# Gate chain of an mLSTM and MoE layer divided anew between engines, with a moved product, other banks, one transpose per tile and another load order

## The reference, cut to what matters

```
h = rmsnorm(x, g_pre_mix) * (1.0 + scale_a) + shift_a
z = h @ w_in                                  # u | q | k | v | o | gate_pre
pre = gate_pre + b_gate
log_i, log_f = pre[i], jax.nn.log_sigmoid(pre[f])     # per direction, head, token
...
b = jnp.cumsum(log_f); m_t = jnp.maximum(b + m, max(b_t - b_s + log_i_s))
p = jnp.exp(d_intra - m_t) * (q @ k)
...
mix = jnp.concatenate([y_pool, y_ml]) @ w_out
x = x + gate_a * rmsnorm(mix, g_post_mix)
x = x + gate_f * rmsnorm(moe(...), g_post_ffn)        # 64 experts, top 6
```

## Time and profile before

| | us |
|---|---|
| median of 3 runs | 725.98 (725.54 to 726.65) |
| the profiled execution | 726.23 |
| its span | 724.10 |
| PE busy, share of the span | 685.0 (95%) |
| DVE, ACT, POOL busy | 384.5, 194.1, 89.1 |
| mean granted TensorE clock | 0.994 of full speed |

### The profile page before, as it was taken

How to read it: one execution, slowest core, us unless ns; L and a number is a source line. 1 busy time by engine, 2 the same in 40 slices (tenths; PEclk the granted TensorE clock), 3 DMA queues, 4 the chain that set the end, 5 groups by cost and what they waited for, 6 DMA issues and landing times.

```text
span 724.1 us, 11495 instructions
## 1 busy us (share of the span) xinstructions
PE 685.0 (95%) x4263; PEld 395.1 (55%) x4263; DVE 384.5 (53%) x979; ACT 194.1 (27%) x335; POOL 89.1 (12%) x53
## 2 busy tenths in 40 slices
PE   2799999989999999999999999999999999999993
PEld 2588888767865735545444545454445445444431
DVE  3458989694298354454444445454445436442115
ACT  3245344563371302112111111211111121130103
POOL 2453655313213000000000000000000000000000
PEclk9999999999999999999999999999999999999997
DMA  9999875815489479999999999999999999999994
GB/s 316 382 350 340 260 245 221 296 55 175 146 329 426 204 290 417 428 423 427 393 386 428 421 425 424 423 425 424 425 424 427 423 425 426 423 426 421 419 410 189
DMA packets 51013, 259.16 MB, mean 358 GB/s; under 512 B 6704, under 2 KB 9312, under 8 KB 32904
## 3 DMA queue, kind: packets, MB, share of 16 engines
q1 hardware_dynamic: 46816, 252.50, 86.6%
q0 software_dynamic: 1584, 4.90, 2.0%
q10 hardware_dynamic: 2552, 0.98, 0.5%
HBM read 254.64 MB, written 3.71 MB: 357 GB/s over the span
## 4 chain that ended last, share of the span: by engine, by line
PE 66%; DMA 14%; DVE 12%; SPq 3%; issue 2%; ACT 2%; POOL 0%; DVEq 0%; ACTq 0%
PE psum L2495 22%; PE psum L2503 10%; PE psum L2383 9%; PE psum L2467 8%; DMA w_gu<-in_w_expert_gu 7%; DVE psum L1329 4%; DMA w_gu<-in_w_in 3%; PE psum L2344 3%; DMA w_dn<-in_w_expert_down 2%; DMA w_gu<-in_w_ada 2%; PE psum L2395 2%; SPq L800 1%; PE psum L604 1%; PE psum L2454 1%; PE psum L2067 1%
## 5 line engine op out<-in xcount | busy, mean ns | idle before, releaser
L2495 PE MATMUL psum<-w_gu,hgT 128*32 128x512 f32 (+1 forms) x1280 | 191.4, 594 | 2.5 <-DMA w_gu<-in_w_expert_gu 2.5
L2495 PEld LDWEIGHTS psum<-w_gu,hgT 128*32 128x32 f32 (+1 forms) x1280 | 57.9, 119 | 127.7 <-issue 127.6
L1782 DVE TENSOR_TENSOR f_acc<-f_acc,psum 128x512 f32<-128x512 f32 x132 | 86.7, 684 | 43.3 <-PE psum L2467 43.3
L2503 PE MATMUL psum<-w_dn,actT 128*32 128x512 f32 (+1 forms) x640 | 98.7, 596 | 1.4 <-DMA w_dn<-in_w_expert_down 0.9
L1760 DVE SCALAR_TENSOR_TENSOR act<-sil,wsl,psum 128x256 f32<-128x256 f32 x27 | 18.4, 681 | 127.6 <-ACT sil L1127 118.3
L589 POOL TENSOR_TENSOR w_lo<-w_gu,w_hi 128x2048 fp32r<-128x2048 f32 x13 | 59.9, 4606 | 71.4 <-ACT w_hi L881 71.4
L2383 PE MATMUL psum<-onehot,h_lo 128*128 128x512 f32 (+1 forms) x168 | 66.6, 397 | 0.0
L2383 PE MATMUL psum<-onehot,h_hi 128*128 128x512 f32 (+1 forms) x168 | 65.4, 389 | 0.0
L2503 PEld LDWEIGHTS psum<-w_dn,actT 128*32 128x32 f32 (+1 forms) x640 | 27.0, 119 | 58.5 <-issue 57.7
L1766 DVE TENSOR_TENSOR y_lo<-psum,y_hi 128x1024 fp32r<-128x1024 f32 x26 | 31.8, 1224 | 50.8 <-ACT y_hi L1131 50.8
L1127 ACT ACTIVATE sil<-psum 128x256 f32<-128x256 f32 x27 | 10.4, 384 | 173.7 <-PE psum L2495 173.7
(11 more groups left out here) (335 smaller groups left out, 846.5 us busy)
## 6 DMA issues: line engine op xcount, KB each, us to landing
w_gu<-in_w_expert_gu SPq DMA_DIRECT2D x49, 2048.0 KB, 17.3
w_dn<-in_w_expert_down SPq DMA_DIRECT2D x61, 1024.0 KB, 15.1
w_gu<-in_w_expert_gu SPq DMA_DIRECT2D x27, 1024.0 KB, 15.9
w_gu<-in_w_ada SPq DMA_DIRECT2D x12, 2048.0 KB, 13.4
w_gu<-in_w_in SPq DMA_DIRECT2D x4, 2048.0 KB, 10.2
w_gu<-in_w_out SPq DMA_DIRECT2D x2, 2048.0 KB, 9.0
bc<-mod_rows POOLq DMA_DIRECT2D x6, 512.0 KB, 7.3
w_gu<-in_w_expert_gu SPq DMA_DIRECT2D x6, 512.0 KB, 20.4
```

What stands on the lines that cost most here:

```text
L1782: v.tensor_tensor(dst, dst, bank(5 + n), ALU.add).then_inc(f_added, 1)
L2495: ins = t.matmul(bank(target)[rows, :], column(c)[:, rows], w_gu[s][:, c, :], start=(c == 0), stop=(c == NC - 1), tile_position=(0, rows.s ...
L2503: ins = t.matmul(bank(target + n)[rows, :], actT[:, j, rows], w_dn[s][:, j, 512 * n:512 * (n + 1)], start=(j == 0), stop=(j == 1), tile_po ...
```

## The change

Six things are edited.

- **The gate chain on ACT and DVE.** DVE writes `g_lf` before `g_in` and signals each piece (`raw_ready`). ACT makes |x| itself. DVE then does min(x, 0) and the subtraction in one operation. `ada_evac(4)` moves ahead of this operation. The negation and the scans stay on DVE.
- **a4's product** stands inside q's second half, ahead of its last pass, writes bank 5, and no longer waits for |x|. `high(3)`, the copy of k's second half, stands between q's second and third copy.
- **k's banks** are 4, 3, 2, 5 (they were 2, 3, 4, 5); v, o and u take 4, 3, 2 (2, 3, 4). k's last unit waits for a4's row to be read.
- **Gate rows in one tile.** `g_nat` is one tile of 72 partitions, zeroed at the start, with u, b and t at partitions 0, 32 and 64. The backward rows are copied by ACT (six copies of 4 partitions), the forward rows by three DMAs that SP issues behind a5 and ahead of a6, after `scans_ready` and `w_ready`. DVE's nine copies are gone. `gates_T` is one matmul of 24 columns per tile; DVE's copy to `gT` is two.
- **ACT's small DMAs** (the final m, and g_post_ffn) are issued behind `high(5)`.
- **a8 ahead of u**: SP issues a8, u, a9 (it was u, a8, a9).

```diff
-        g_nat = at("g_nat", [36, 3, T], BC + 15104)
+        g_nat = at("g_nat", [72, T], BC + 17408)
...
-            j = 3 if i == 4 else i % 4
-            return bank(6 + i % 2, P * j, P * j + P)
+            return bank(5, 0, P) if i == 4 else bank(6 + i % 2, P * (i % 4), P * (i % 4) + P)
...
-            return (1, 2, 0, 7)[i] if w == "q" else 2 + i
+            return {"q": (1, 2, 0, 7), "k": (4, 3, 2, 5)}.get(w, (4, 3, 2))[i]
...
-            issued = ["a0", "a2", "q", "a1", "a3", "q", "k", "a4", "v", "a5", "a6", "o", "a7"] + order[chunk["u"]:]
+            issued = ["a0", "a2", "q", "a1", "a3", "q", "k", "a4", "v", "a5", "a6", "o", "a7"] + ["a8", "u", "a9"] + order[chunk["w0"]:]
...
+                if name == "a5":
+                    sp.wait_ge(scans_ready, 1)
+                    sp.wait_ge(w_ready, 2)
+                    for n, rows in enumerate((g_u, g_b, g_t)):
+                        sp.dma_start(g_nat[32 * n + H:32 * n + 2 * H, :], rows[0:H, :]).then_inc(nat_ready, 16)
...
-            a.wait_ge(abs_ready, 1)
+            a.wait_ge(raw_ready, NT + 1)
+            own.link(a.activation(g_t[:, :], g_lf[:, :], ACT.Abs))
             own.link(a.activation(g_t[:, :], g_t[:, :], ACT.Exp, scale=-1.0))
             a.activation(g_t[:, :], g_t[:, :], ACT.Ln, bias=1.0).then_inc(soft_ready, 1)
-            for n in range(4):
-                z_evac(n)
+            z_evac(0)
+            z_evac(1)
             high(3)
+            z_evac(2)
+            z_evac(3)
...
+            a.wait_ge(w_ready, 2)
+            for n, rows in enumerate((g_u, g_b, g_t)):
+                here = slice(32 * n, 32 * n + H)
+                a.activation(g_nat[here, 0:T_CTX], rows[32:36, natural(1, 0)], ACT.Copy).then_inc(nat_ready, 1)
+                a.activation(g_nat[here, T_CTX:T], rows[32:36, T - 1:T_CTX - 1:-1], ACT.Copy).then_inc(nat_ready, 1)
...
+            ada_evac(4)
+            v.wait_ge(raw_ready, 2 * (NT + 1))
             v.wait_ge(soft_ready, 1)
-            own.link(v.tensor_tensor(g_lf[:, :], g_lf[:, :], g_t[:, :], ALU.subtract))
+            own.link(v.scalar_tensor_tensor(g_lf[:, :], g_lf[:, :], 0.0, g_t[:, :], ALU.min, ALU.subtract))
...
                 q_high_low(range(H), 1)
+                ada(4)
                 q_low(range(H), 1)
...
+                        if (w, half, i) == ("k", 0, H - 1):
+                            t.wait_ge(mod_ready, 5)
...
-                t.wait_ge(nat_ready, 9)
-                for a_ in range(3):
-                    col = T + 24 * a_ + 8 * tile
-                    ins = t.matmul(bank(1, col, col + 2 * H), g_nat[:, a_, P * tile:P * tile + P],
-                                   ident[0:36, 0:64].rearrange("p (d r) -> p d r", d=2)[:, :, 0:H],
-                                   start=True, stop=True)
-                ins.then_inc(gT_done, 1)
+                t.wait_ge(nat_ready, 6 + 16 * 3)
+                col = T + 24 * tile
+                t.matmul(bank(1, col, col + 24), g_nat[:, P * tile:P * tile + P],
+                         ident[0:72, 0:96].rearrange("p (a r) -> p a r", a=3)[:, :, 0:2 * H],
+                         start=True, stop=True).then_inc(gT_done, 1)
```

More of the change, by code:

```diff
@@ L436, in build_layer @@
         gate_part_ready = sem("gate_part_ready")
-        abs_ready, soft_ready, scans_ready, w_ready, nat_ready = (
-            sem("abs_ready"), sem("soft_ready"), sem("scans_ready"), sem("w_ready"), sem("nat_ready"))
+        raw_ready, soft_ready, scans_ready, w_ready, nat_ready = (
+            sem("raw_ready"), sem("soft_ready"), sem("scans_ready"), sem("w_ready"), sem("nat_ready"))
         gT_done, gT_ready, em_ready, ktok_done, ktok_ready = (
@@ L938, in _ @@
             a.activation(g_t[:, T_CTX:T], g_lf[:, T_CTX:T], ACT.Exp, bias=m0).then_inc(w_ready, 1)
+            a.wait_ge(w_ready, 2)
[3 more added lines that the diff above has]
+                a.activation(g_nat[here, T_CTX:T], rows[32:36, T - 1:T_CTX - 1:-1], ACT.Copy).then_inc(nat_ready, 1)
+            high(4)
+            for n in range(4, 8):
+                z_evac(n)
+            high(5)
             for d in range(2):
@@ L945, in _ @@
                     .then_inc(grow2_in, 16)
[L946 to L949, removed]
             high(6)
@@ L953, in _ @@
             high(7)
-            a.wait_ge(gT_ready, 1)
+            a.wait_ge(gT_ready, 2)
             a.activation(emT[:, :, :], gT[:, 1, :, :], ACT.Exp, scale=-1.0).then_inc(em_ready, 1)
@@ L1236, in _ @@
             own.add(v.memset(gate_sum[:, :], 0.0))
+            own.add(v.memset(g_nat[:, :], 0.0))
             own.add(v.memset(v1[:, :, :, DH:DV], 1.0))
@@ L1315, in ada_sums @@
                         v.wait_ge(z_act, 4)
-                        v.wait_ge(mod_ready, 5)
                     elif i == 9:
@@ L1333, in _ @@
             v.wait_ge(gates_done, 3)
-            for b, dst in enumerate((g_in, g_lf)):
-                own.add(v.tensor_scalar(dst[0:32, :], bank(6, 0, T)[64 * b:64 * b + 32, :], b_gate[0:32, b:b + 1], None, ALU.add))
+            for b, dst in ((1, g_lf), (0, g_in)):
+                v.tensor_scalar(dst[0:32, :], bank(6, 0, T)[64 * b:64 * b + 32, :], b_gate[0:32, b:b + 1], None, ALU.add)\
+                    .then_inc(raw_ready, 1)
                 for tile in range(NT):
[L1337 to L1343, removed]
+                    v.tensor_scalar(dst[32:36, P * tile:P * tile + P],
+                                    bank(6, 0, T)[64 * b + 32:64 * b + 36, natural(1, tile)],
+                                    b_gate[32:36, b:b + 1], None, ALU.add).then_inc(raw_ready, 1)
+            ada_evac(4)
+            v.wait_ge(raw_ready, 2 * (NT + 1))
             v.wait_ge(soft_ready, 1)
-            own.link(v.tensor_tensor(g_lf[:, :], g_lf[:, :], g_t[:, :], ALU.subtract))
+            own.link(v.scalar_tensor_tensor(g_lf[:, :], g_lf[:, :], 0.0, g_t[:, :], ALU.min, ALU.subtract))
             SEG = ((0, T_CTX), (T_CTX, T))
@@ L1356, in _ @@
             v.tensor_tensor(g_b[:, :], g_b[:, :], g_mx[:, :], ALU.add).then_inc(scans_ready, 1)
-            ada_evac(4)
             ada_sums(5)
[L1359 to L1364, removed]
             ada_sums(6)
@@ L1367, in _ @@
             v.wait_ge(gT_done, NT)
-            v.tensor_copy(gT[:, :, :, :].rearrange("p a i r -> p (a i r)"), bank(1, T, T + 72)).then_inc(gT_ready, 1)
+            rows_T = bank(1, T, T + 72).rearrange("p (i a r) -> p a i r", i=NT, a=3)
+            for d in range(2):
+                v.tensor_copy(gT[:, :, :, H * d:H * d + H], rows_T[:, :, :, H * (1 - d):H * (1 - d) + H]).then_inc(gT_ready, 1)
             ada_evac(5)
@@ L2003, in ada @@
                     t.wait_ge(mod_ready, max(i - 1, 4))
-                if i == 4:
-                    t.wait_ge(abs_ready, 1)
                 if i > 4:
@@ L2021, in ada_total @@
                 if i >= 6:
-                    t.wait_ge(gT_ready, 1)
+                    t.wait_ge(gT_ready, 2)
                 for m in range(2):
@@ L2193, in _ @@
                     z_chunk(w)
-                if w == "q":
-                    ada(4)
                 if w == "o":
```

1 line of the change is left out of this document (removed).

## The result

| | before | after |
|---|---|---|
| median, us | 725.98 (725.05 to 726.65, 13 runs) | 728.22 (726.36 to 730.98, 13 runs) |
| profiled execution | 726.23, span 724.10 | 727.79, span 725.5 |
| mean granted TensorE clock | 0.994 | 0.990 |

The ratio is 1.0033, with a 95% interval of 1.0022 to 1.0044: the change made the kernel 2.2 us slower. The forecast was 723.2 us, faster, with a range of 721.4 to 727.0. Both the time and the sign were wrong.

The account below looks back on a forecast made before the run. The prediction took PE (66% of the span) as the bound; -1.88 - 1.35 + 0.9 - 0.45 = -2.78 us gave 723.2 us against the median of 725.98. The range was 721.4 to 727.0 us.

Parts of the forecast that it names:

- PE at the start of k: Before k: a4's product moved into q removes two PE idle pieces, 0.64 and 1.24 us; -1.88 us.
- Transposes: Gate-row transposes at three places between v's units: one matmul left of three, 0.45 us saved each; -1.35 us.
- The gate chain: DVE and ACT gate work: scans_ready falls from 65.8 to 58.3 us, passing POOL's next difference with 0.3 us to spare.
- the second rival: Gate chain on DVE: it starts after POOL's difference, is locked, and delays o; 726.4 us, chance 0.20 with its twin.
- SP's added wait: SP's queue behind a5: waiting for gate rows delays a6, constants and o; PE waits +0.9 us, bounds 0 to +4.4.
- the twin of the second rival: SP's queue: its 17 us at the constants do not shrink, so o is late; 726.6 us, within the shared 0.20 chance.
- The third rival: SP's queue: late a6 plus the full 17 us, o issued at 83.2; +3.9 us in all, 729.9 us, chance 0.07.
- rule of where o lands: o's weights: landing later than 88.5 us eats the gain; later than 90 makes the kernel slower by over 0.2%.
- PE's idle before o over 3 us: Sign before o's first product: PE idle above 3 us would show the forecast wrong; about 1 us was expected.
- total(9): End of the stretch: ada_total(9) no longer waits for a9's sums, saving -0.45 of PE's 0.51 us wait.
- first rival: o's weights arrive in time, so PE does not wait before o: -3.7 us, 722.3 us, chance 0.17.

Follow-up runs that it names:

- The best experiment: Changed kernel with the last four constants issued behind u and the gate-row copies issued by ACT without SP's wait: 721.18 us, ratio 0.9933 to the kernel before.
- the last three runs: Last four constants moved: changed kernel, behind u, 722.30 us; the same with rows issued by ACT, 721.18; kernel before, behind a8, 726.54.
- the last control: Kernel before the change with only its last four constants issued behind a8 and ahead of a9: 726.54 us, ratio 1.0011.
- its two controls: Kernel before with all seven constants behind v, 725.65 us (ratio 0.9996), and with only the last four behind a8, 726.54 us (1.0011).

## Why the prediction was wrong, point by point

**PE at the start of k: right.** -1.88 was put down. k starts 2.61 us sooner, 0.72 of it the lead: -1.89. k's own stage gave a further 0.21 that was not in the sum.

**Transposes: right in kind, too small.** -1.35 was put down, 0.45 a place, with the entry into the small shape staying. From the last product ahead of a place to the second behind it the time fell from 1.42 (85.56 to 86.98) to 0.69 us (82.64 to 83.33), 0.73 at each of the first two places. At the third it fell by 0.62, and v's start gave 0.11, together -2.18. The entry shrank too. This made PE want o sooner, so while o was late the error was worth nothing.

**The gate chain: right.** |x| was at 49.56 (50.2 forecast), the operation behind L1354 took 0.35, and the locked one with two inputs ended behind POOL's difference as put down. The slack against POOL was 0.05 us, not 0.3, and the second rival's mechanism did not occur. a5's sums began at 64.05 (63.9 forecast; with the lead taken out 64.8, since a5 landed 8.5 us after its issue and not 7.9). a7's began at 93.35 (near 91) and a9's ended at 128.5 (124.5), which PE did not wait for.

**SP's added wait: the step that failed.** It stood in the sum with +0.9, bounds 0 to +4.4; it measured +4.9. Counted from the start of the gates on DVE, which takes the lead out (48.65 before, 47.93 after), o was to be issued 27.75 us later and was 30.4 later: +2.6. One us of that is ahead of a6, mostly the three row copies at 0.58 to 0.78 each instead of 0.43. The other 1.6 lie between a6 and o: 15.75 us instead of 14.1. The argument was that the stand at pool_scale is a full queue and shrinks if the queue is emptier. It shrank from 8.14 to 7.01, and then w_router took 3.10 where it had taken 1.71. The forecast let a6's bytes end 2.1 us later than before; with the lead taken out a6 landed 3.3 us later (71.5 against 68.9). The landing of o took 9.6 instead of 9.2, and PE wanted o 41.7 us behind the start of the gates instead of 42.75, because the steps above gave more than forecast. 0.9 + 2.6 + 0.4 + 1.0 is 4.9. Of the cases put down, the twin of the second rival is the nearest: o issued at 79.9, w_lo ready at 95.8, time 726.6. With the lead taken out o was issued at 79.0 and w_lo was ready at 95.2, and without the clock's loss the kernel took 725.90. The third rival's lateness (o at 83.2) came by less than half. Its rule of where o lands (later than 88.5 eats the gain) would have called 87.9, or 88.6 with the lead taken out, a draw.

**The clock: missing from the text.** No term and no rival had the granted clock in it. It cost 2.3 us, and turned a draw into a loss: without it the changed kernel measured 725.90, beside 726.3 for the one before. The sign of the result hangs on this. The prediction named "PE's idle before o over 3 us" as what would prove it wrong, but priced that idle at its own length.

**total(9): right.** -0.45 was put down. DVE's release with its wait of 0.51 is gone, a gap of 0.16 is left, and the step from total(8) to total(9) is 0.35 shorter.

**The rest of the sum.** Take o's stop and the clock away, and -1.89 - 0.21 - 2.18 - 0.35 = -4.6 is left. The best experiment measured -4.6 too. The forecast's first rival, with o in time, had -3.7.

**What stays open.** Why pool_scale, with 512 single values, holds SP so long was not tested. The traces show a regularity. In all ten kernels in which it stands right behind the three large constants it took 5.7 to 8.6 us, and SP was free 0.5 to 0.9 us after the last 2 MB block ahead of the constants had landed:

| last block ahead of the constants | landed | SP free |
|---|---|---|
| a6, the kernel before | 68.9 | 69.57 |
| a6, changed | 71.5 | 72.25 |
| a7, all constants behind it | 86.1 | 86.70 |
| u, all constants behind it | 100.1 | 100.66 |
| v, all constants behind it | 55.0 | 55.52 |

Without the large constants ahead of it (the last three runs) it took 3.55, 1.81 and 2.50 and was not held until a landing. So the hold goes with what is queued ahead. The seven together do take less when they start later: 19.4 us from 56.61 without SP's wait, 15.0 from 63.23 with it. The forecast had this direction right and took too much for it. What in the queue makes SP wait isn't shown. Three of the twelve runs of the last control took over 728 us at a mean clock of 0.993, and were not profiled, so where their clock fell isn't known.

## What to carry to other kernels

A load's lateness is not priced at PE's idle time alone: the stops of 2.4 and 4.8 us here cost a further 1.7 and 2.3 us at the lower clock behind them, so a forecast needs a second term for the clock. When PE is made faster, first reckon for each block of weights when it is issued, lands and is wanted; the one with the least slack takes the gain, and moving a long row of small loads only hands the delay to the next block unless it fits into a gap of the issuing queue. Split such a row, and keep only as much of it ahead of the critical load as the slot's own wait covers.

## What the runs showed of the hardware

- The granted clock against the length of PE's stop, all in this stretch: 0.9 and 1.1 us left it at 1.00. 2.4 us brought a mean of 0.68 over the 4 us behind it. 4.8 and 5.7 us brought 0.50 while PE still stood; PE went on at 94.49 and 113.67, and 1.00 was back from 100 and from 117 us. 3.0 us at total(9), with short products behind it, brought 0.80 over 6 us and 0.63 over the next 6.
- Five otherwise useless matmuls in the stop were worth 2.3 us in the medians, which is all of the clock's loss in the ledger (2.29).
- Three kernels whose longest stop was 0.3 to 1.1 us repeated within 1.1 to 1.8 us (5 to 10 runs, mean clock 0.994 to 0.996 in each). With a stop of 2.4 us ten runs spread over 6.1 us. The short stops alone don't settle the spread: the kernel before and its two controls have stops of 1.2 us and spread over 1.6 to 3.4 us (10 to 27 runs).
- The seven constants, 2.3 MB with most bytes in the first three, held SP 15.0 us behind a6 in the changed kernel (17.0 in the kernel before, 19.4 without SP's wait), 15.8 behind a7, 16.6 behind u and 20.6 behind v. The number of values doesn't set it: pool_scale has 512 and state_n 1,024, and took 7.01 and 2.37 us.
- DVE's operation with one SBUF input took 0.35 us and its last one 0.55 when both stood just ahead of POOL's difference; the first took 4.79 when it started 0.02 us behind one.
